# Products of constants on TensorE in front of the waits at sub-layer boundaries

## The reference

```python
def _sub_in(x, mod, i, g_pre):
    return _rmsnorm(x, g_pre) * (1.0 + mod[:, i, 1][:, None]) + mod[:, i, 0][:, None]

def _sub_out(x, mod, i, g_post, out, res_w):
    return x + res_w * (1.0 + mod[:, i, 2][:, None]) * _rmsnorm(out, g_post)

for li in range(DEPTH):
    mod = _ada(c, w_ada[li], b_ada[li])            # silu(c) @ w + b
    h = _sub_in(x, mod, 0, norm_pre[li, 0])
    x = _sub_out(x, mod, 0, norm_post[li, 0], _swiglu(h, wg, wu, wd), 0.5)
    h = _sub_in(x, mod, 1, norm_pre[li, 1])
    out = mixer(h)          # li 0: attention in chunks (A) and differential (B); li 1: forgetting (C)
    x = _sub_out(x, mod, 1, norm_post[li, 1], out, 1.0)
    h = _sub_in(x, mod, 2, norm_pre[li, 2])
    x = _sub_out(x, mod, 2, norm_post[li, 2], _swiglu(h, wg2, wu2, wd2), 0.5)
```

## Time and profile before

| | |
|---|---|
| median of 3 runs | 2628.42 us |
| profiled execution | 2632.73 us, span 2630.9 us |
| PE busy | 2425.5 us, 92% |
| VectorE busy | 1552.9 us, 59% |
| ScalarE busy | 856.0 us, 33% |
| mean granted TensorE clock | 0.957 of full speed |
| PE waits for h_lo (line 1784) | 56.6 us in 33 waits |
| PE waits for x_slot (line 1629) | 26.9 us in 9 waits |

### The profile page before, as it was taken

One profiled execution on the slowest core, in us unless ns is written; L12 is line 12 of the kernel. 1 busy time (PEld: TensorE's weight loads), 2 busy tenths in 40 slices (PEclk: granted clock), 3 DMA queues, 4 the chain that ended last, 5 costly groups with the idle time before them and its releaser, 6 DMA issues. The chain is left out here.

```text
span 2630.9 us, 44404 instructions
## 1 busy us (share of the span) xinstructions
PE 2425.5 (92%) x18216; PEld 2316.4 (88%) x18216; DVE 1552.9 (59%) x2767; ACT 856.0 (33%) x1764; POOL 338.3 (13%) x426
## 2 busy tenths in 40 slices
PE   7999999889997799999979999986999886999997
PEld 6999999878885699999969999985888786999997
DVE  3377768655556756667574665756555557443323
ACT  2222222344544332222232222233444443222222
POOL 0000002421011500001230000233011133000002
PEclk9999999889997899999989999997999988999999
DMA  6255545322222124454413554532233221342331
GB/s 222 66 161 168 169 135 162 97 60 68 69 66 69 36 86 141 137 152 141 133 49 105 152 148 130 149 96 67 73 92 91 73 59 49 110 121 84 87 87 62
DMA packets 392697, 277.59 MB, mean 106 GB/s; under 512 B 11104, under 2 KB 349824, under 8 KB 392496
## 3 DMA queue, kind: packets, MB, share of 16 engines
q1 hardware_dynamic: 385792, 254.77, 32.9%
q0 software_dynamic: 6704, 19.99, 2.6%
HBM read 263.48 MB, written 12.81 MB: 105 GB/s over the span
## 5 line engine op out<-in xcount | busy, mean ns | idle before, releaser
L894 PE MATMUL lin<-h_hi,w_hi 128*128 128x272 f32 x2720 | 600.2, 293 | 36.6 <-DVE h_lo L1784 36.4
L894 PE MATMUL lin<-h_hi,w_lo 128*128 128x272 f32 x2720 | 592.4, 291 | 0.0
L894 PE MATMUL lin<-h_lo,w_hi 128*128 128x272 f32 x2720 | 590.9, 290 | 0.0
L1629 DVE TENSOR_TENSOR w_lo<-raw,w_hi 128x1024 fp32r<-128x1024 f32 (+1 forms) x270 | 329.3, 1224 | 290.3 <-ACT w_hi L1266 289.4
L894 PEld LDWEIGHTS lin<-h_hi,w_hi 128*128 128x128 f32 x2720 | 442.2, 190 | 44.9 <-DVE h_lo L1784 28.8
L894 PEld LDWEIGHTS lin<-h_lo,w_hi 128*128 128x128 f32 x2720 | 443.4, 191 | 0.3
L894 PEld LDWEIGHTS lin<-h_hi,w_lo 128*128 128x128 f32 x2720 | 440.6, 191 | 0.0
L1266 ACT ACTIVATE w_hi<-raw 128x1024 fp32r<-128x1024 f32 (+1 forms) x270 | 276.3, 1032 | 181.9 <-DMA raw<-in_ffn_w_down 151.0
L1668 DVE SCALAR_TENSOR_TENSOR acc<-raw,silu_c,acc 128x512 f32<-128x512 f32 x448 | 313.1, 758 | 0.0
L894 PE MATMUL lin<-act_hi,w_hi 128*128 128x272 f32 x1296 | 286.4, 292 | 6.6 <-DVE w_lo L1629 6.4
L894 PE MATMUL lin<-act_hi,w_lo 128*128 128x272 f32 x1296 | 283.4, 289 | 0.0
(11 more groups left out here) (260 smaller groups left out, 3542.3 us busy)
## 6 DMA issues: line engine op xcount, KB each, us to landing
raw<-in_w_ada SPq DMA_DIRECT2D x128, 512.0 KB, 3.8
raw<-in_ffn_w_gate SPq DMA_DIRECT2D x88, 512.0 KB, 3.8
raw<-in_ffn_w_up SPq DMA_DIRECT2D x88, 512.0 KB, 3.8
raw<-in_ffn_w_down SPq DMA_DIRECT2D x64, 448.0 KB, 4.1
raw<-in_ffn_w_down SPq DMA_DIRECT2D x32, 512.0 KB, 4.7
raw<-in_w_in_ab SPq DMA_DIRECT2D x24, 512.0 KB, 3.8
raw<-in_w_in_c SPq DMA_DIRECT2D x24, 512.0 KB, 3.9
start_w<-in_w_ada SPq DMA_DIRECT2D x16, 512.0 KB, 12.4
```

The source lines that it names most:

```text
L894: m = nc.tensor.matmul(out[a], w[:, k, :], mv[:, k0 + k, half(a)], start=first and k == 0 and n == 0, stop=last and k == u["tiles"] - 1 an ...
L1629: nc.vector.tensor_tensor(w_l[:, 0:u["tiles"], :], raw[:, u["slot"], 0:u["tiles"], 0:w_l.shape[-1]], w_h[:, 0:u["tiles"], :].bitcast(F32), ...
```

## The change

TensorE gets `fill(n)`: n products of two constants, the identity `ident` and `mean_w`, each 128x128 by 128 columns in plain float32, written to the bank `ps_o` and read by nobody. They stand in the first chunk of either half of each head (8 in front of the first k-tile, 4 in front of each later one), in front of the three slot chunks of half 0 in ffn heads (6, 4, 4), and 8 behind the last mean of the program. A head now also waits at its start for the coefficients of all jobs before it.

```diff
--- before.py
+++ after.py
@@ -39,6 +39,9 @@
 START = (0, 2, 1, 3)
 NJOB = 2 * 9 * DM // JOB
 HEAD = 3
+IDLE_FIRST = (8, 4)
+IDLE_SLOT = (6, 4, 4)
+IDLE_END = 8
 DCH = ((0, 8), (8, 7), (15, 7))
 ONCE = {"ffn": 6, "ab": 2, "c": 2}
 POOL_X = {"ffn": (4, 5, 6, 7), "ab": (6, 7), "c": (6, 7)}
@@ -878,14 +881,25 @@
         def _(pe):
             steps = [0]
 
-            def chunk(name, halves, out, hi, lo, k0=0, first=True, last=True, gradual=None, mid=None):
+            def fill(n, bank=ps_o):
+
+                for _ in range(n):
+                    nc.tensor.matmul(bank[:, 0:P], ident[:], mean_w[:], start=True, stop=True)
+
+            def jobs_before(j):
+                return len(START) + sum(len(q[i]) for q in (GU_JOBS, DN_JOBS) for i in q if i < j)
+
+            def chunk(name, halves, out, hi, lo, k0=0, first=True, last=True, gradual=None, mid=None, idle=(0, 0)):
 
                 u = U[name]
+                if gradual is None:
+                    fill(idle[0])
                 if ws.count[name, halves[0]] == min(ws.count[name, 0], ws.count[name, 1]):
                     pe.wait_ge(lo_done, u["idx"] + 1)
                 w_h, w_l = slot_hi[u["hl"]], slot_lo[u["hl"]]
                 for k in range(u["tiles"]):
                     if gradual is not None:
+                        fill(idle[0] if k == 0 else idle[1])
                         pe.wait_ge(h_lo_done, gradual + k + 1)
                     if mid is not None and k == mid[0]:
                         mid[1]()
@@ -948,9 +962,16 @@
 
                 names = head_order(kind, j)
                 prev = j - 1
+                if j > 0:
+                    pe.wait_ge(job_coef, jobs_before(j))
                 for a in (0, 1):
                     for i, name in enumerate(names):
                         mid = None
+                        idle = (0, 0)
+                        if j > 0 and i == 0:
+                            idle = IDLE_FIRST
+                        elif j > 0 and kind == "ffn" and a == 0 and i >= 3:
+                            idle = (IDLE_SLOT[i - 3], 0)
                         if a == 0 and j > 0:
                             at = (0, 5) if KIND[prev] == "ffn" else (1, 2)
                             if at[0] == i:
@@ -976,7 +997,7 @@
                             else:
                                 pe.wait_ge(kv_evac, ev + k + 1)
                             out = {a: lin[0:16, b, 0:HALF] if k is None else bank(b)}
-                        chunk(name, (a,), out, h_hi, h_lo, gradual=2 * KT * j + KT * a if i == 0 else None, mid=mid)
+                        chunk(name, (a,), out, h_hi, h_lo, gradual=2 * KT * j + KT * a if i == 0 else None, mid=mid, idle=idle)
 
             def gate_up(j):
                 base = ITEMS * ffn_index(j)
@@ -1240,6 +1261,7 @@
 
 
             mean(NSUB - 1, 1)
+            fill(IDLE_END)
             for n, (a, t) in enumerate(nat_order):
                 for h in range(1 if t < 2 else 2):
                     by_pool, by_dve = x_adds(NSUB - 1, h, 4 * a + 3)
```

## The result

The changed kernel takes 2654.61 us (median of 4 runs, 2651.86 to 2657.21), the kernel before 2629.26 (2628.07 to 2632.04) beside it: a ratio of 1.0092, 95% interval 1.0076 to 1.0108. It is slower by some 25 us. The profiled execution took 2653.31 us with a span of 2651.4, against 2632.73 and 2630.9: 20.5 us more in the span.

What follows compares the result with a forecast made beforehand. TensorE, busy 92%, bounds sub-layers; in the five heads it waits for h_lo and weight slots. Terms 4.8 + 5.1 + 6.8 + 2 + 1.8 + 0.8 = 21.3 us, against the 2628.42 median, gave 2650 us; range 2640 to 2661.

Steps and rivals of the forecast that it cites:

- The price of a fill: Each 128x128 by 128 f32 product on TensorE costs 0.22 us at full clock, 0.43 at half clock.
- The rival with one short record per fill: A fill is a single record of 0.11 us on TensorE, so the kernel takes 2635 us; chance 0.06.
- Half 1 of the ffn heads: First chunks there take 10.9 us, fills having nothing to hide in: head 3 +4.8, head 2 +5.1, head 5 +6.8 us.
- Third slot chunk at half clock: In heads 2, 3 and 5 it may still start at half clock, costing 1.5 to 2.4 us; at one in three, +2.
- Half 0 of the ffn heads: Slot-chunk fills hide in waits; TensorE reaches half 1 at 932.8 instead of 935.56 (head 2), 1371.6 instead of 1374.50 (head 3).
- the first rival: Second halves do wait and their fills are hidden; only gains of 2 and 3.3 us in heads 2 and 3 stay: 2623; chance 0.04.
- Head 1: Half 1 begins 0.5 us later, its first chunk takes 11.1 us with half clock at first; the head costs +1.8 us.
- Head 4: Half 1 starts from a late DMA without shift, its first chunk takes 11.1 us, partly at half clock; +0.8 us.
- The end and the wait on job_coef: The 8 fills at the end cost 0, at most 1.8 us; waiting for coefficients at a head's start costs nothing.
- The signs named: Ffn half 1: no h_lo waits, chunks about 11 us; heads 1 to 4: mean ends 0 to 1.2 us earlier; heads 2, 3: higher clock.
- The rival of no hold on the clock: Fills don't hold the clock; each half's first chunk takes 21.0 us at half clock, kernel 2700 us; chance 0.04.
- The faster rival: In the heads' second halves TensorE waits and fills are hidden, so the kernel takes 2623 us; chance 0.04.

Runs made afterwards that it cites:

- fills only where TensorE waits: Changed kernel without fills in half 1 of ffn heads, and with 8 then 2 per later tile in half 1 of heads 1 and 4: 2630.21 us, ratio 0.9987.

## Why the prediction was right

Forecast 2650 us from a sum of +21.3; measured 2654.61, and +20.5 in the profiled span. The mechanism held: fills where TensorE has no wait are paid in full, and those in half 1 of the ffn heads are the loss. Some of the closeness is luck, and is marked so. Point by point, in profiled executions:

- **The price of a fill**, 0.22 us: 0.223 from half the dose in three heads. Right. The rival with one short record per fill fell: the kernel has 820 records. With transposes, which are such records, the ratio falls from 1.0092 to 1.0038, some 14 us, where that rival's arithmetic had 11.9 and about 3 more.
- **Half 1 of the ffn heads.** Chunks of 10.9 us were forecast, 11.04 to 11.06 came, with no wait for h_lo. Head 2 +5.09 (5.1 forecast), head 3 +5.26 (4.8), head 5 +8.88 (6.8 and a share of the next term; 0.3 of the miss is that the first chunk of half 1 had ended at 2231.3 before, not at 2231.6). That these 108 fills make the loss is shown from both sides: with them alone 1.0082, without them, but with every other place filled in some dose, 0.9987.
- **Third slot chunk at half clock**, +2 in all at one in three: it happened in head 5 alone, where half 0 ended 1.6 us later than before (44.20 against 42.57 us from the head's start). Without that delay head 5 would be at +7.25. That one head in three met it is a chance that came out as put, and no reading: in the other kernels with the changed kernel's fills up to half 1 it happened in none (half 0 only), in head 5 (half the dose in half 1; 24 fills in the mixers) or in heads 2 and 5 (fills only where TensorE waits).
- **Half 0 of the ffn heads.** It ended 2.9 us (head 2) and 2.4 us (head 3) earlier. The terms of the sum had 2.8 (935.56 to 932.8) and 2.9 (1374.50 to 1371.6); the first rival puts the same gains at 2 and 3.3, which does not agree with them. Right in size, though the shares by cause were not measured apart.
- **Head 1.** +1.27 against +1.8. Half 0 ended 0.5 later and the root for half 1 (now line 1335) started 0.55 later, both as forecast. But half 1 did not begin later for it, as the forecast had it: VectorE started the first h_lo at the same distance from the head's start as before, and the first pass came 0.1 earlier (30.65 against 30.75). That is the 0.5 missing. Half 1 itself took 17.15 us against 17.1 forecast. Half clock in it came 1.4 us after the first pass and lasted from 532.71 to 536.13, 3.4 us, where the forecast had 4.2 from the first pass on.
- **Head 4.** 0.0 against +0.8, by two misses that cancel, which is luck. The mean began 1.9 us later (14.89 us from the head's start against 12.97) and its last record 0.8, which I had put at nothing; half 1's first pass came 0.45 later. And half 1 ran at full clock from its first pass, where I had taken half clock: 18.84 us against 19.33. TensorE waits there twice: first until VectorE has read the forget gate's sums (z_t), then for h_lo. The eight fills stand between the two waits. The waits in head 4 and the timeline of the changed kernel show it:

```profile
PE ps_o L887 <- DVE z_t L2137: 3.8, 1, 3.8
...
1809.34 3.65 PE L887 MATMUL ps_o<-mean_w,ident 128*128 128x128 f32 x16 [3.75 <-DVE z_t L2137]
1813.74 0.30 PE L908 MATMUL lin<-h_hi,f_slot 128*16 128x272 f32 x1 [0.76 <-DVE h_lo L1806]
```

  They cover nothing of the first wait and run slowly themselves (16 records in 3.65 us), but in time that was idle before, when the whole wait was 9.09 us. Half 1 then ran at full clock (1.00), and nearly or wholly so with fewer fills there (0.96 and 1.00 with 8 and 2; head 4 -1.4 and -1.3), but not without any (0.68 in the kernel with fills in half 0 only; head 4 +0.7). With 24 fills there and none between tiles it was 1.00 too. So these fills, unlike those in the ffn heads, did pay for themselves.

- **The end and the wait on job_coef**: nothing forecast. The last mean came 20.2 us later than before and the last TensorE work 20.4 later, so the end added 0.2; no row shows a wait for the coefficients.
- **The signs named.** Half 1 without waits, chunks of 11 us and a higher clock in heads 2 and 3 came. The last record of the mean started 0.7, 1.1 and 0.4 us earlier in heads 1 to 3, as said, but 0.8 later in head 4.
- **The rival of no hold on the clock** fell with the granted clock (0.75 to 0.96 in head 3). The faster rival, that fills in half 1 are hidden, fell with the windows without idle time.

The forecast sum was 21.3 and the profiled spans differ by 20.5, while the medians differ by 25.4. By the numbers that is which execution was profiled: that of before lay 3.5 us above its median, that of the changed kernel 1.3 below. The forecast put the sum of +21.3 on the median of 2628.42, and so it is 4.6 low. What the other executions did otherwise no trace shows.

What stays open: why the third slot chunk meets half clock in one kernel and not in another with the same fills before it, and why the stretches between the heads differ. The one moves 1 to 2 us a head, the other up to 2.8 us a stretch, and both are as large as the gain that the best variants show.

The four variants without fills in half 1 of the ffn heads and with fills before the slot chunks (0.9986 to 0.9990) are not told apart by their intervals. They lie 0.1% under the kernel before, with upper bounds of 0.9995 to 1.0000, and the changed kernel 0.9% above it. Fills in half 0 only (0.9989) is the simplest of them.

## What to carry to other kernels

A product that keeps the clock up is paid for at the full rate wherever the engine had no wait: count the fills in each place, multiply by the start-to-start distance, and compare with the idle time of that place and not of the kernel. More clock is not less time: with long slot fills 89 us of half clock fewer (137 instead of 226) came with a ratio of 0.9990. In head 3 the last step, from 0.92 to 1.00, was worth nothing. That VectorE or a weight slot sets the end of most such stretches fits this and was not measured stretch by stretch. Put a fill in front of the wait that it is to cover, and see in the timeline which of several waits that is.

## What the runs showed of the hardware

- An f32 transpose of 128x128 costs 0.11 us and is one record, an f32 product of the same size 0.22 and two records; with the same engine time and number of records they did much the same for the granted clock in this kernel (0.92 and 0.96 in head 3, 0.78 and 0.77 with half).
- With half of every dose head 3 up to half 1 came out at 0.77, hardly above the 0.75 without any fill, and with the full dose at 0.96.
- The clock dropped behind 5.5 us of uninterrupted fills in head 1 (533.65 to 543.89), while PE ran a chunk whose tiles came one at a time: here a covered wait did not protect the stretch behind it.
- In head 4, eight fills between two waits and four before each later k-tile, or 24 between the waits alone, went with full clock in the whole of half 1 (1.00), where it was 0.68 without fills there.
